# Projection, norm, router and shared expert in one block by token tile; row sums of the last stage on TensorE with diagonal weights

## What is computed

```python
x = layer_norm(DN_ALPHA * x + gate1 * merge_branches(y_a, y_b, y_c, zg, p), p['ln1_g'], p['ln1_b'])
h = x * (1.0 + scale2) + shift2
x = layer_norm(DN_ALPHA * x + gate2 * moe_ffn(h, p), p['ln2_g'], p['ln2_b'])
...
    return merged @ p['w_out']
...
    scores = jax.nn.sigmoid((x @ p['router_w']).astype(F32))
...
    y_sh = (jax.nn.silu(x @ p['sh_w_gate']) * (x @ p['sh_w_up'])) @ p['sh_w_down']
    return (y + y_sh).reshape(shape)
```

## Time and profile before

| | us |
|---|---|
| median of 3 runs | 2528.96 (2528.1 to 2529.77) |
| the profiled execution's own time | 2519.51 |
| its span, first to last instruction | 2517.7 |
| projection block | 1641.4 to 1769.2 |
| router block | 1770.1 to 1872.5 |
| expert jobs | 1873.3 to 2386.1 |
| last stage | 2393.6 to 2517.7 |

### The profile page before, as it was taken

The page is one execution under the profiler, slowest core; times in us unless marked ns, Lnnn a source line. Parts: engine busy times, 40 slices in busy tenths (PEclk is TensorE's granted clock), DMA queues, the critical chain, the costliest instruction groups (busy, mean ns, idle before and its releaser), DMA issues. The chain is left out here.

```text
span 2517.7 us, 41126 instructions
## 1 busy us (share of the span) xinstructions
PE 2066.8 (82%) x16339; PEld 1575.7 (63%) x16339; DVE 933.0 (37%) x1863; ACT 491.8 (20%) x928; POOL 685.4 (27%) x1030
## 2 busy tenths in 40 slices
PE   7989879979769989999999975975829999999800
PEld 7666545546548777777777765932528888877600
DVE  0734221207624444333454332734251222222267
ACT  0211122112123233232332312100102222212100
POOL 4416000000013233232332211312013444444423
PEclk9989878789989898888998887997769999999955
DMA  7233344545131120211210016600128998999572
GB/s 236 67 117 101 122 138 139 175 173 191 59 115 52 44 73 19 59 57 34 66 40 24 7 49 246 214 33 18 45 73 323 334 322 305 334 341 323 211 308 100
DMA packets 244753, 358.31 MB, mean 142 GB/s; under 512 B 38305, under 2 KB 173236, under 8 KB 240772
## 3 DMA queue, kind: packets, MB, share of 16 engines
q1 hardware_dynamic: 216734, 299.42, 35.2%
q0 software_dynamic: 24560, 45.27, 5.0%
q10 hardware_dynamic: 3318, 11.59, 1.3%
HBM read 308.42 MB, written 85.65 MB: 157 GB/s over the span
## 5 line engine op out<-in xcount | busy, mean ns | idle before, releaser
L440 PE MATMUL ps_s<-hT,w_in_sb 128*128 128x512 f32 x432 | 214.6, 654 | 0.0
L2688 DVE TENSOR_TENSOR me_hh<-me_sg,ps_ju 128x128 f32<-128x128 f32 x76 | 21.9, 288 | 398.8 <-PE ps_jd L2645 375.3
L1262 PE MATMUL ps_gs<-hT,gt_w 128*128 128x512 f32 x256 | 147.6, 660 | 11.0 <-PEq L75 7.3
L440 PEld LDWEIGHTS ps_s<-hT,w_in_sb 128*128 128x128 f32 x432 | 89.9, 214 | 105.1 <-issue 104.9
L2637 PE MATMUL ps_jg<-me_xT,me_wg 128*128 128x128 f32 x1216 | 149.0, 276 | 0.0
L2637 PE MATMUL ps_ju<-me_xT,me_wu 128*128 128x128 f32 x1216 | 148.2, 275 | 0.0
L2645 PE MATMUL ps_jd<-me_wd,me_hh 128*128 128x512 f32 x304 | 143.9, 596 | 2.4 <-DVE me_yb L2694 2.4
L2637 PEld LDWEIGHTS ps_jg<-me_xT,me_wg 128*128 128x128 f32 x1216 | 142.7, 193 | 0.1
L2637 PEld LDWEIGHTS ps_ju<-me_xT,me_wu 128*128 128x128 f32 x1216 | 141.9, 192 | 0.0
L2666 ACT ACTIVATE me_xT<-ps_jx 128x1024 f32<-128x1024 f32 x77 | 78.9, 1024 | 256.7 <-PE ps_jx L2628 256.7
L2628 PEld LDWEIGHTS ps_jx<-ident,me_xg 128*128 128x128 f32 x616 | 79.4, 192 | 72.2 <-DMA me_xg<-h_dram,me_ids 43.1
(11 more groups left out here) (536 smaller groups left out, 4207.3 us busy)
## 6 DMA issues: line engine op xcount, KB each, us to landing
me_wg<-in_exp_w_gate SPq DMA_DIRECT2D x76, 512.0 KB
me_wu<-in_exp_w_up SPq DMA_DIRECT2D x76, 512.0 KB
me_wd<-in_exp_w_down SPq DMA_DIRECT2D x76, 512.0 KB
cb_rows<-yj_dram SPq DMA_DIRECT2D x10, 2048.0 KB
w_ad_sb<-in_w_ada SPq DMA_DIRECT2D x32, 512.0 KB
w_in_sb<-in_w_in SPq DMA_DIRECT2D x31, 512.0 KB
gt_w<-in_w_in SPq DMA_DIRECT2D x24, 512.0 KB, 4.1
zr<-in_w_ada SPq DMA_DIRECT2D x4, 2048.0 KB, 10.6
```

The costliest lines, as they stand in the source:

```text
L440: mm(ps_s[:, b, :], w_in[:, r, k, :], hT[:, k, 0:TS], start=(k == 0), stop=(k == KT - 1))
L1262: nc.tensor.matmul(ps_s[:], w[:, t % WR, k, :], hT[:, k, 0:TS], start=(k == 0), stop=(k == KT - 1))
```

## The change

`residual_router_phase` takes the place of both phases. Tile by tile, PE projects, turns and makes logits. The choice of experts is cut into three parts of 2, 2 and 1 tiles. The shared expert's up projection runs for the first 512 tokens ahead of the last tile's turning; its down projection stands behind the counts. The one-hot tables are made with three wide instructions per tile, in the memory of `wo` and `mT`, and PE takes each tile's as it comes. The gates' `pick` goes to the start of the expert jobs on DVE, and the loads of `g2` and of the last norm's vectors to ACT's queue there. In the last stage PE sums the first BYPE = 6 of 8 rows of a token, with diagonal matrices of gates that POOL makes; DVE adds the other two and PE's sum.

```diff
-        hot_p, hot_j = sb("ro_hotp", [P, NT * TOPK, P]), sb("ro_hotj", [P, NT * TOPK, JCOLS])
+        hot_p = wo[:].rearrange("p k c -> p (k c)")[:, 0:NT * TOPK * P].rearrange("p (q c) -> p q c", q=NT * TOPK)
+        hot_j = mT[:].rearrange("p k n -> p (k n)")[:, 0:NT * TOPK * JCOLS].rearrange("p (q c) -> p q c", q=NT * TOPK)
...
+        ps_j = ps_t[:, 0, :]
+        pg = {(0, 0): ps_o[:, 1, 0:TS], (1, 0): ps_o[:, 1, TS:2 * TS], (0, 1): ps_o[:, 0, 0:TP], (1, 1): ps_o[:, 0, TS:TS + TP]}
...
+                def logits(t):
+                    if t == 0:
+                        pe.wait_ge(m.t_w, 16)
+                    pe.wait_ge(m.o_ht, 2 * t + 2)
...
+                def shared_up(c):
+                    if c == 0:
+                        pe.wait_ge(m.u_w, 32)
+                    pe.wait_ge(m.o_tp, NT - 1 + c)
+                    for n, w in ((0, wg), (1, wu)):
                         for k in range(KT):
...
+                            last = mm(pg[n, c], w[:, k, :], m.h2T[:, k, halves[c]], start=(k == 0), stop=(k == KT - 1))
+                    last.then_inc(m.u_up, 1)
+                pe.wait_ge(m.o_w, 16 * FT)
                 for t in range(NT):
-                    for h in range(2):
-                        n = 2 * t + h
-                        if n >= 2:
-                            pe.wait_ge(m.u_acc, n - 1)
-                        mm(pd[:, h, :], hh[:, t * P:(t + 1) * P], wd[:, ts512(h)], start=True, stop=True).then_inc(m.u_dn, 1)
-
-                pe.wait_ge(m.t_ch, 1)
+                    project(t)
+                    if t:
+                        turn(t - 1)
+                    if t >= 2:
+                        logits(t - 2)
+                logits(NT - 2)
+                shared_up(0)
+                turn(NT - 1)
+                logits(NT - 1)
+                shared_up(1)
+
+                pe.wait_ge(m.t_ch, len(SELECT))
...
+                pe.wait_ge(m.u_wd, 16)
+                pe.wait_ge(m.u_hh, 2)
...
+                for t in range(NT):
+                    pe.wait_ge(m.t_hot, t + 1)
+                    for j in range(TOPK):
+                        q = t * TOPK + j
+                        last = mm(ps_j[:, 0:JCOLS], hot_p[:, q, :], hot_j[:, q, :], start=(q == 0), stop=(q == NT * TOPK - 1))
...
+                def scored(t0, t1):
+                    act.wait_ge(m.t_mm, t1)
+                    A(sc[:, t0:t1], ps[:, t0:t1], ACT.Sigmoid).then_inc(m.t_sc, 1)
+                for t in range(NT):
+                    rooted(t)
+                    if t:
+                        turned(t - 1)
+                    if t == 3:
+                        scored(0, 2)
+                scored(2, 4)
+                turned(NT - 1)
+                scored(4, 5)
...
+                def select(i):
+
+                    t0, t1 = SELECT[i]
+                    n, T = t1 - t0, slice(t0, t1)
+                    dve.wait_ge(m.t_sc, i + 1)
...
+                for t in range(NT - 1):
+                    residual(t)
+                    if t:
+                        modulate(t - 1)
+                select(0)
+                residual(NT - 1)
+                modulate(NT - 2)
+                modulate(NT - 1)
+                select(1)
+                select(2)
+                dve.wait_ge(m.t_ch, len(SELECT))
...
-                for t in range(NT):
-                    last = V.tensor_tensor(pick[:, t], slot[:, t].unsqueeze(1).to_broadcast([P, TOPK, E_N]),
-                                           top[:, t].unsqueeze(2).to_broadcast([P, TOPK, E_N]), ALU.is_equal)
...
-                for t in range(NT):
-                    last = V.tensor_tensor(pick[:, t], pick[:, t], gates[:, t].unsqueeze(1).to_broadcast([P, TOPK, E_N]), ALU.mult)
...
-                V.tensor_reduce(m.gj[:], pick[:], AX.X, ALU.add)
...
-                for q in range(NT * TOPK):
-                    t, j = q // TOPK, q % TOPK
-                    V.tensor_scalar(hot_p[:, q, :], col[:], place[:, t, j:j + 1], None, ALU.is_equal)
-                    last = V.tensor_scalar(hot_j[:, q, :], col[:, 0:JCOLS], job[:, t, j:j + 1], tok[:, q:q + 1],
-                                           ALU.is_equal, ALU.mult)
-                last.then_inc(m.t_hot, 1)
+                dve.wait_ge(m.o_mm, NT)
+                for t in range(NT):
+                    Q = slice(t * TOPK, (t + 1) * TOPK)
+                    V.tensor_tensor(hot_p[:, Q, :], col[:].unsqueeze(1).to_broadcast([P, TOPK, P]),
+                                    place[:, t, :].unsqueeze(2).to_broadcast([P, TOPK, P]), ALU.is_equal)
+                    link(V.tensor_tensor(hot_j[:, Q, :], col[:, 0:JCOLS].unsqueeze(1).to_broadcast([P, TOPK, JCOLS]),
+                                         job[:, t, :].unsqueeze(2).to_broadcast([P, TOPK, JCOLS]), ALU.is_equal))
+                    V.tensor_tensor(hot_j[:, Q, :], hot_j[:, Q, :], tok[:, Q].unsqueeze(2).to_broadcast([P, TOPK, JCOLS]),
+                                    ALU.mult).then_inc(m.t_hot, 1)
...
+                for c in range(2):
+                    act.dma_start(m.g2[:, c], m.mods_dram[c, GATE2 * D:(GATE2 + 1) * D].partition_broadcast(P)).then_inc(m.j_vec, 16)
+                act.dma_start(m.ln2g[:], a["ln2_g"].partition_broadcast(P)).then_inc(m.j_vec, 16)
+                act.dma_start(m.ln2b[:], a["ln2_b"].partition_broadcast(P)).then_inc(m.j_vec, 16)
                 run(act, group)
+                act.wait_ge(m.j_vec, 64)
...
+                plink = Chain(dve, m.j_pick)
+                for t in range(NT):
+                    last = V.tensor_tensor(pick[:, t], m.slot[:, t].unsqueeze(1).to_broadcast([P, TOPK, E_N]),
+                                           m.top[:, t].unsqueeze(2).to_broadcast([P, TOPK, E_N]), ALU.is_equal)
+                plink(last)
+                for t in range(NT):
+                    last = V.tensor_tensor(pick[:, t], pick[:, t], m.gates[:, t].unsqueeze(1).to_broadcast([P, TOPK, E_N]), ALU.mult)
+                plink(last)
+                V.tensor_reduce(m.gj[:], pick[:], AX.X, ALU.add)
                 end = run(dve, group)
...
-                        sp.wait_ge(m.e_used, (q - NR + 1) * HALF)
+                        t, h = (q - NR) // 2, q % 2
+                        sp.wait_ge(m.e_mm, 2 * t + h + 1)
+                        if h:
+                            sp.wait_ge(m.e_used, (t + 1) * (TOPK - BYPE))
...
+                def weights(t):
+
+                    if t >= 2:
+                        pool.wait_ge(m.e_mm, 2 * (t - 1))
+                    nc.gpsimd.tensor_tensor(diag[:, t % 2], m.ident[:].unsqueeze(1).to_broadcast([P, BYPE, P]),
+                                            m.gj[:, t, 0:BYPE].unsqueeze(2).to_broadcast([P, BYPE, P]), ALU.mult).then_inc(m.e_dg, 1)
+                for t in range(2):
+                    weights(t)
...
                     o = a["y_prompt"] if t == NT - 1 else a["y_sample"][t * P:(t + 1) * P, :]
                     pool.dma_start(o, m.acc[:, t]).then_inc(m.e_out, 16)
+                    if t + 2 < NT:
+                        weights(t + 2)
...
+                for t in range(NT):
+                    pe.wait_ge(m.e_dg, t + 1)
+                    if t >= 2:
+                        pe.wait_ge(m.e_sum, t - 1)
+                    for j in range(BYPE):
+                        b = piece(t, j)
+                        if j % HALF == 0:
+                            pe.wait_ge(m.e_land[b % NR], 16 * (b // NR + 1))
+                        for h in range(2):
+                            last = nc.tensor.matmul(ps[:, t % 2, ts512(h)], diag[:, t % 2, j, :], rows[:, b % NR, j % HALF, ts512(h)],
+                                                    start=(j == 0), stop=(j == BYPE - 1))
+                        if j == HALF - 1 or j == BYPE - 1:
+                            last.then_inc(m.e_mm, 1)
...
-                    for j in range(TOPK):
...
+                    for j in range(BYPE, TOPK):
+                        b, n = piece(t, j), t * (TOPK - BYPE) + j - BYPE
...
+                        if j > BYPE:
+                            dve.wait_ge(m.e_used, n)
                         V.scalar_tensor_tensor(x, rows[:, b % NR, j % HALF], m.gj[:, t, j:j + 1], x, ALU.mult, ALU.add).then_inc(m.e_used, 1)
-                    dve.wait_ge(m.e_used, (t + 1) * TOPK)
-                    if t == 0:
-                        dve.wait_ge(m.e_g, 64)
+                    dve.wait_ge(m.e_used, (t + 1) * (TOPK - BYPE))
+                    dve.wait_ge(m.e_mm, 2 * t + 2)
+                    V.tensor_tensor(x, x, ps[:, t % 2], ALU.add).then_inc(m.e_sum, 1)
+                    dve.wait_ge(m.e_sum, t + 1)
```

327 lines of the change are left out of this document (141 added, 186 removed).

## The result

The changed kernel took 2457.96 us in the median of four runs (2454.63 to 2466.0), the kernel before 2528.53 us beside it (four runs, 2523.01 to 2529.77). The ratio is 0.973 with a 95% interval of 0.970 to 0.976. The forecast was 2456 us.

What follows compares the result with a forecast made beforehand. Before the last stage PE and DVE wait for each other; there DVE sets the end. Gains of 41.4 and 33.4 less 2.0 us give 72.8, so 2528.96 - 72.8 = 2456.2 us; range 2440 to 2480.

Steps and rivals of the forecast that it cites:

- Part 1, the merged block: Projection, router and shared expert merged: `row` made at 1830.4 instead of 1871.81, 41.4 us less, range 34 to 47.
- the counts: Merged block, PE behind the choice of experts: 40 records at full clock, 4.3 us, with the handover 4.6.
- Part 2, the start of the jobs: Start of the expert jobs with pick and early loads: 2 us more, range 0 to 9.
- the collision that was priced at 1.5 us: Start of the expert jobs: POOL's short instructions wait for DVE's pick passes, first gather late by 0 to 3.5 us.
- Part 3, the last stage: Row sums moved to PE, vectors loaded early: first gate product 5.7 us earlier, later tiles 27.7 us less, gain 33.4 us.
- PE: 10.4 us per tile of 13.7, with sums in two buffers, so it isn't late: Last stage: PE's sums need 10.4 us of a 13.7 us tile, not late even after losing 2 us to the clock.
- a period over 16 us: Last stage: sign that would make the prediction wrong; 13.7 us from gate product to gate product was expected.
- No exclusion: Last stage: DVE and POOL don't exclude each other, PE binds at 10.4 us per tile, 11.7 us more gained: 2444.5; chance 0.12.
- PE at half clock through the last stage: Last stage: PE stays at 1.2 GHz, 20.6 us per tile, a loss of 3 us instead of a gain: 2492.6; chance 0.07.
- A dearer start of the jobs: Expert jobs: pick wholly on the path (9.0) and extra loads too (5.0), 12 us more than priced: 2468; chance 0.08.
- A block that overlaps less than written: Merged block: last tile's choice waits behind up projection, ACT's table changes and POOL, 8 to 12 us lost: 2466; chance 0.09.
- Slower everywhere: Merged block and last stage: low clock persists through wide matmuls, 10.5 us slower than before: 2539.5; chance 0.02.

Runs made afterwards that it cites:

- the old start: Kernel before with only the last stage's change and its early vector loads, pick and router as before: ratio 0.988 to the kernel before.
- the second trace: The changed kernel unaltered, profiled once more: 807.7 us from the first projection to the end, ratio 0.973 to the kernel before.
- the weights first: Changed kernel with the diagonal weights of all five tiles made by POOL at the last stage's start, ahead of every norm pass: ratio 0.969 to the kernel before.

## Why the prediction was right, and where it was not

**Part 1, the merged block: right, by its steps.** Forecast 189.0 us to `row`, measured 189.6. On the way, counted from the first projection: turning of tile 3 at 126.9 forecast and 126.7 measured; end of the big up projection 151.3 and 150.6; choice done 160.6 and 160.1; counts handed over 165.6 and 166.8; first one-hot 169.8 and 171.2; `row` 189.0 and 189.6. The term that was off by most is the counts, 4.6 us forecast: they took 6.5, at a mean clock of 0.69, behind a wait of 2 us.

```profile
1781.80:1788.50 6.70, 6.70 (x34) 6.70 (x33) 2.45 (x2) 1.88 (x2) 0.40 (x1) 0.50 0.23 95
1813.40:1819.90 6.50, 6.46 (x41) 6.47 (x41) 1.83 (x5) 0.00 (x0) 0.00 (x0) 0.69 0.00 0
```

That the logits between the projections are on the path was right (moving them made `row` 9.1 us earlier). That they would be slow was right too, but it was only half understood: the pause ahead of them loses the clock, and matmuls of the same width right behind a projection keep it.

**Part 2, the start of the jobs: right, at the low side.** Forecast 2 us more, with a range to 9. From the row to PE's first turning it was 0.6 to 0.9 us more (14.27 before, 15.12 and 14.91 after). From there to DVE's first product it was another 1.0 to 1.1 us more (9.98 before, 10.99 and 11.08 after). That is not shown to be the loads: without them it took 11.07 us, with them and the old start 10.06, and 9.3 to 11.1 in all fourteen traces. POOL's three short instructions ahead of the first gather took 0.66, 0.64 and 0.53 us beside the pick, where the next ones take 0.2: the collision that was priced at 1.5 us costs 0.5 to 1. The jobs' own length, 1.2 and 3.5 us over before's in the two traces, lies in the spread of single executions.

**Part 3, the last stage: right in kind, 4.4 us too good in size, by one step.** Forecast 33.4 us, measured 29.0, and 29.8 in the second trace (*end* 105.2 against 135.0). The first gate product came 22.2 us after the stage's start (22.6 forecast), the tile that waited for nothing took 13.28 us (13.7), the tail 14.8 as before. The step that failed is "PE: 10.4 us per tile of 13.7, with sums in two buffers, so it isn't late". It compared rates and left out when PE may begin. The weights of tile t+2 stand on POOL behind tile t's passes and output; I had put their time into DVE's period, at 9.5 us behind the norm, and not asked who waits for them. PE began tile 2 at 10.0 us behind tile 0's norm, needed 12.4 us at the clock it had lost, and DVE, due for the sum 18.6 us behind that norm, waited 3.9. From the first gate product to the last it took 58.0 us for 53.3. The three waits add up to 9.2 us and cost only 4.7 against the forecast, mainly because in the two tiles that waited long DVE's gate and residual steps stood clear of POOL and took 1.22 us each instead of 2.0 and 2.4. From gate product to gate product the tiles took 11.3, 17.2, 11.5 and 18.1 us; a period over 16 us was one of the signs on record that would make the prediction wrong, and for this step it did. PE's clock, expected near 1 from the second tile on, fell to 0.66 over 10 us behind two of the waits. With the weights first the time from the first gate product to the last became 47.5 us, below my number too, because my period also held the collision with the weights.

**The rivals.** No exclusion: refuted, by the kernel without POOL's passes. PE at half clock through the last stage: no, 0.79 in the mean, high from the first tile on, and lost again for a time behind waits for weights. A dearer start of the jobs: no. A block that overlaps less than written: no. Slower everywhere: no; each stretch of wide matmuls recovered its clock.

**The median.** The forecast lies 1.8 us from the measured median, nearer than its parts were, and that closeness is in part luck. The trace of before was of an execution 9.45 us shorter than the median, and I carried that distance over; the medians lie 70.6 us apart where 72.8 were forecast. By ratios the change was forecast at 0.971 and measured at 0.973. The profiled executions, 53.5 us apart, would have given a worse answer than either: their untouched parts differ by 12 us.

## What to carry to other kernels

When work moves to an idle engine, ask of every operand it needs which instruction makes it, and what that instruction stands behind on its own engine; a rate of 10.4 against 13.7 us says nothing while the operand comes only 10 us behind the norm. Things that depend on nothing late (here five sets of weights) belong ahead of the loop, which was worth 9 to 10 us of a stage of 95. In a latency-bound block, work that nobody waits for (the shared expert here) belongs into the gaps, and what the next chain waits for goes ahead of it: the same matmuls in another order gave 20 us.

## What the runs showed of the hardware

- POOL's passes slow DVE instructions with two SBUF inputs and are slowed by them: two DVE rows that take 2.67 us without the passes took 4.57 us beside them, and a POOL pass of 2.33 became 3.33 us. The starts and ends fit an exclusion with the first come in front, and either can be the one that pays: with one row, started ahead of the pass, the row took 1.28 us and the pass 3.33. DVE's sum with one input in PSUM kept its 1.22 us in every tile of every kernel.
- Matmuls of 64 columns kept a high clock and did not raise a low one: 5.47 us for three tiles of logits at clock 1.00 right behind a projection, 3.67 us for one tile at 0.50 behind a wait of 4.72 us, and 17.3 us for five tiles at 0.50 to their end before the change. A wait of 4.14 us between the down projection and the jobs' first turning was enough to lose it.
- 2 MB more for the DMA engines, in a loop where they are 90% busy, could not be told from none (0.962 with and without).
